# First mixer: norm with one root per token, gate bias loaded early, first projection k by k, five modulation blocks a slab

## The reference

```
def modulate(x, g, shift, scale):
    return rms_norm(x, g) * (1.0 + scale) + shift
...
        mod = (silu_c @ w_mod[l] + b_mod[l]).reshape(B, 3 * N_SUB, 1, D)
        x = macaron_half_ffn(x, norm_g[l, 0], *mod_terms(mod, 0), ffn_w_in[l, 0], ffn_w_out[l, 0])
        sh, sc, gt = mod_terms(mod, 1)
        h = modulate(x, norm_g[l, 1], sh, sc)
...
            y, yx = even_mixer(h, hx, mix_w_in[e], na_rpb[e], ml_gate_b[e], ml_head_g[e], mix_w_out[e], ctx_out)
```

## Time and profile before

| | |
|---|---|
| median of 3 runs | 2561.55 us (2555.28 to 2567.85) |
| the profiled execution | 2558.21 us, its span 2556.4 us |
| PE busy | 2424.2 us, 95% |
| DVE busy | 1718.7 us, 67% |
| ACT busy | 1191.6 us, 47% |
| chain that ended last, by engine | PE 70%, DVE 16%, ACT 9% |
| DMA | 501.16 MB, 196 GB/s on average |

### The profile page before, as it was taken

One profiled execution on the slowest core, in us unless ns is written; L12 is line 12 of the kernel. 1 busy time (PEld: TensorE's weight loads), 2 busy tenths in 40 slices (PEclk: granted clock), 3 DMA queues, 4 the chain that ended last, 5 costly groups with the idle time before them and its releaser, 6 DMA issues.

```text
span 2556.4 us, 34122 instructions
## 1 busy us (share of the span) xinstructions
PE 2424.2 (95%) x14294; PEld 2078.5 (81%) x14294; DVE 1718.7 (67%) x2273; ACT 1191.6 (47%) x1523; POOL 98.9 (4%) x187
## 2 busy tenths in 40 slices
PE   7999999898989999999999999989999899899997
PEld 3778888667789999998899997767777777678776
DVE  5997776653766656655556655577887684678776
ACT  3222222333554544446344444465766644566665
POOL 0111111010000000000000000000000000000000
PEclk9999999999999999999899999999999996999999
DMA  6777787322124545465245542257887521388774
GB/s 274 231 238 263 264 265 252 132 79 94 67 100 167 184 178 179 168 224 191 105 149 177 189 174 102 99 184 271 335 323 293 211 94 53 138 309 329 295 289 175
DMA packets 80386, 501.16 MB, mean 196 GB/s; under 512 B 9605, under 2 KB 10709, under 8 KB 28497
## 3 DMA queue, kind: packets, MB, share of 16 engines
q1 hardware_dynamic: 59120, 423.66, 45.1%
q0 software_dynamic: 21088, 75.01, 9.2%
HBM read 497.58 MB, written 1.05 MB: 195 GB/s over the span
## 4 chain that ended last, share of the span: by engine, by line
PE 70%; DVE 16%; ACT 9%; issue 3%; DMA 2%; ACTq 0%; DVEq 0%; SPq 0%
PE bank L402 68%; DVE wl L1957 7%; ACT wh L1340 6%; DVE macc L1993 1%; ACT s L1438 1%; DVE f L2152 1%; PE bank L613 1%; DVE s L2143 1%; DVE rs L2017 1%; PE bank L1234 1%; DMA raw<-in_wstream 1%; DMA raw<-in_wmod 1%; DMA mring<-in_wmod 1%; DVE hl L2127 0%; ACT H L1447 0%
## 5 line engine op out<-in xcount | busy, mean ns | idle before, releaser
L1957 DVE TENSOR_TENSOR wl<-raw,wh 128x2048 fp32r<-128x2048 f32 (+1 forms) x432 | 903.8, 2097 | 410.7 <-ACT wh L1340 407.8
L1340 ACT ACTIVATE wh<-raw 128x2048 fp32r<-128x2048 f32 (+1 forms) x432 | 755.3, 1756 | 365.2 <-PE bank L402 349.3
L402 PE MATMUL bank<-hh,wh 128*128 128x258 f32 (+2 forms) x2200 | 696.6, 317 | 31.6 <-DVE wl L1957 7.7
L402 PE MATMUL bank<-hh,wl 128*128 128x258 f32 (+2 forms) x2200 | 676.8, 308 | 0.0
L402 PE MATMUL bank<-hl,wh 128*128 128x258 f32 (+2 forms) x2200 | 675.4, 307 | 0.0
L402 PEld LDWEIGHTS bank<-hh,wh 128*128 128x128 f32 x2200 | 424.2, 193 | 62.0 <-DVE hl L2127 8.1
L402 PEld LDWEIGHTS bank<-hl,wh 128*128 128x128 f32 x2200 | 424.8, 193 | 18.5
L402 PEld LDWEIGHTS bank<-hh,wl 128*128 128x128 f32 x2200 | 422.8, 192 | 18.9
L402 PE MATMUL bank<-wh,hh 128*128 128x512 f32 (+1 forms) x704 | 277.9, 395 | 5.5 <-DVE hl L2903 2.8
L402 PE MATMUL bank<-wh,hl 128*128 128x512 f32 (+1 forms) x704 | 273.4, 388 | 0.0
L402 PE MATMUL bank<-wl,hh 128*128 128x512 f32 (+1 forms) x704 | 273.3, 388 | 0.0
(11 more groups left out here) (437 smaller groups left out, 2678.1 us busy)
## 6 DMA issues: line engine op xcount, KB each, us to landing
raw<-in_wstream SPq DMA_DIRECT2D x393, 1024.0 KB, 4.9
mring<-in_wmod POOLq DMA_DIRECT2D x128, 512.0 KB, 4.6
raw<-in_wmod SPq DMA_DIRECT2D x6, 1024.0 KB, 7.1
X<-in_xT SPq DMA_DIRECT2D x1, 2048.0 KB, 12.4
mods<-in_wmod SPq DMA_DIRECT2D x2, 1024.0 KB, 18.9
bias<-in_nabias POOLq DMA_DIRECT2D x16, 128.0 KB, 2.5
c_sglg<-in_sglg POOLq DMA_DIRECT2D x1, 1024.0 KB, 4.5
c_sglb<-in_sglb POOLq DMA_DIRECT2D x1, 1024.0 KB, 6.6
```

Source lines behind the costliest of these rows:

```text
L402: return e.matmul(out, lhsT, rhs, start=start, stop=stop, skip_group_check=True)
L1340: e.activation(wh[i % NB][:, o], raw[i % NR][:, o], ACT.Copy).then_inc(*slab_high(st.split + m))
L1957: e.tensor_tensor(wl[i % NB][:, o], raw[i % NR][:, o], wh[i % NB][:, o].bitcast(F32), ALU.subtract).then_inc(*slab_low(st.split + m))
```

## The change

1. The squares of the mixer's norm are summed with ones as a single column, so that a token's sum stands on its partition (`token_square`, 128x4 in all). `token_inverse` takes mean, root and reciprocal of 128x4, writes them on the diagonal of `rs`, and PE spreads them with one product by ones (`token_roots`). DVE reads the result in its PSUM bank.
2. `naq` is made with k outside: for each k the four column chunks, in four banks.
3. DVE and PE take five modulation blocks at each slab boundary in place of four. All 128 are then through at slab 26 in place of 32, and no sum is left behind the feed-forward.
4. `gateb`, the gates' bias, is loaded with the first constants.
5. ACT's softplus (Abs, Exp, Ln) stands behind the first two of four slab splits, and Ln behind the third.

```
...
@@ -172,6 +172,7 @@
     bmod = const(ctx, "bmod", [P, 2, 72])
     ng = const(ctx, "ng", [P, 7, KC])
     lng = const(ctx, "lng", [P, 8, KC])
+    gate_bias = const(ctx, "gateb", [P, 1])
 
     early = ExitStack()
     macc = sb(early, "macc", [P, 2, 2, D])
...
@@ -421,7 +421,7 @@
             if at == 0:
                 if st.host and i:
                     mod_sums()
-                    mods.advance(4)
+                    mods.advance(5)
                 order.append([])
                 if i:
                     w.wait_ge(slab_low, "slab", i)
@@ -506,14 +506,23 @@
             st.kept.remove(bank_of["ssq", nm])
 
 
-        def first_square(k):
+        def token_square(nm, k):
             if k == 0:
-                st.ssq = bank(("ssq", 0), dve_out, "mean", 0)
+                st.ssq = bank(("ssq", nm), dve_out, "mean", nm)
+                st.kept.add(bank_of["ssq", nm])
                 w.wait_ge(dve_out, "ones")
-            w.wait_ge(act_out, "square", 0, k)
+            w.wait_ge(act_out, "square", nm, k)
             for c in range(4):
                 ins = mm(st.ssq[:, c:c + 1], sq[:, k % 2, P * c:P * c + P], ones[:, 0:1], k == 0 and c == 0, k == KC - 1)
-            ins.then_inc(*result("ssq", 0, k))
+            ins.then_inc(*result("ssq", nm, k))
+            if k == KC - 1:
+                st.kept.remove(bank_of["ssq", nm])
+
+
+        def token_roots(nm, by, *drained):
+            b = bank(("roots", nm), by, *drained)
+            w.wait_ge(dve_out, "diag", nm)
+            mm(b[:], ones[:], rs[:], True, True).then_inc(*result("roots", nm))
 
         def first_mods():
             rows = [bank(("row", i), act_out, "held", i) for i in range(3)]
...
@@ -719,7 +729,12 @@
             def h(k):
                 return h_of(1, 2, k)
 
-            project("min", 4, 0, T, lambda k: h_of(1, 1, k), dve_out, "naq")
+            bs = [bank(("naq", m), dve_out, "naq", m) for m in range(4)]
+            for k in range(KC):
+                w.wait_ge(dve_out, *h_of(1, 1, k))
+                for m, b in enumerate(bs):
+                    wmm(("min", m, k), b[:, 0:T], hh[:, k, 0:T], hl[:, k, 0:T], k == 0, k == KC - 1, "naq", m)
+            st.kept.remove(bank_of["roots", 1])
             project_tok("min", 8, 512, 4, h, act_out, "nav")
 
             def logits(u, kd, qb, hd, b):
@@ -1301,9 +1316,8 @@
         st.host = True
         ffn(1, 0)
         st.host = False
-        mods.advance(200)
-        mod_sums()
-        norm_began(1)
+        token_roots(1, dve_out, "tmp", 1, 2 * KC - 1)
+        st.kept.add(bank_of["roots", 1])
         mixer0()
         ffn(2, 2)
         ffn(3, 3)
...
@@ -1515,15 +1529,16 @@
             w.wait_ge(result, "mixer0 phase 1")
             b = banks[bank_of["mgate", 0]]
             for d in range(2):
-                act(ml.IR[:, d, :], b[32 * d:32 * d + 4, :], ACT.Identity, bias=ml.gb[32 * d:32 * d + 4, :], key=("mgate i", d))
-                act(ml.FR[:, d, :], b[64 + 32 * d:68 + 32 * d, :], ACT.Identity, bias=ml.gb[64 + 32 * d:68 + 32 * d, :],
+                act(ml.IR[:, d, :], b[32 * d:32 * d + 4, :], ACT.Identity, bias=gate_bias[32 * d:32 * d + 4, :], key=("mgate i", d))
+                act(ml.FR[:, d, :], b[64 + 32 * d:68 + 32 * d, :], ACT.Identity, bias=gate_bias[64 + 32 * d:68 + 32 * d, :],
                     key=("mgate", d - 1))
             pad()
+            taken(4 * KC)
             act(ml.t1[:], ml.FR[:], ACT.Abs, key=("softplus", 0))
             act(ml.t1[:], ml.t1[:], ACT.Exp, scale=-1.0, key=("softplus", 1))
+            taken(2 * KC)
             act(ml.t1[:], ml.t1[:], ACT.Ln, bias=1.0, key=("softplus", 2))
-            taken(4 * KC)
-            taken(4 * KC)
+            taken(2 * KC)
             for step in range(4):
                 for d in range(2):
                     ch = seqs[d][step]
@@ -1918,7 +1933,8 @@
         first_mods()
         norm(0, [(0, 0, 1), (2, 0, 1)], ffns[1].tmp)
         ffn(1, 0)
-        root(1, 2 * T)
+        w.wait_ge(dve_out, "mean", 1)
+        e.activation(rt[:], rt[:], ACT.Sqrt).then_inc(*act_out("root", 1))
         norm(1, [(0, 3, 4), (2, 3, 4)], tmpm, 1)
         act_out.mark("mixer0 norm")
         mixer0()
@@ -1963,7 +1979,7 @@
             for i in range(-(-st.tile // 4), -(-(st.tile + n) // 4)):
                 if st.host and i and i % 4 == 0:
                     mod_sums()
-                    for n_ in mods.advance(4):
+                    for n_ in mods.advance(5):
                         mod_block(n_)
                 if st.fine or i % 4 == 0:
                     split_upto(i + 4 * NB - 3 if st.fine else i + 4 * NB)
@@ -2016,6 +2032,17 @@
             for i, o in enumerate(range(0, n, T)):
                 e.reciprocal(rs[:, o:o + T], rs[:, o:o + T]).then_inc(*dve_out("rs", nm, i))
 
+
+        def token_inverse(nm):
+            w.wait_ge(result, "ssq", nm, KC - 1)
+            e.tensor_scalar(rt[:], banks[bank_of["ssq", nm]][:, 0:4], 1.0 / D, 1e-6, ALU.mult, ALU.add).then_inc(*dve_out("mean", nm))
+            w.wait_ge(act_out, "root", nm)
+            e.reciprocal(rt[:], rt[:]).then_inc(*dve_out("inverse", nm))
+            w.wait_ge(const_in["ident"], 0)
+            behind()
+            e.tensor_tensor(rs[:].rearrange("p (b t) -> p b t", b=4), bc(ident[:], 4), rt[:].unsqueeze(2).to_broadcast([P, 4, P]),
+                            ALU.mult).then_inc(*dve_out("diag", nm))
+
         def first_mods():
             e.memset(ones[:], 1.0).then_inc(*dve_out("ones"))
             for k in range(KC):
...
@@ -2104,7 +2124,8 @@
                     behind()
                     e.scalar_tensor_tensor(GV[:, wi, :], mvec(row, scale), 1.0, ng[:, g, :], ALU.add, ALU.mult).then_inc(*dve_out("gv", nm, wi))
             if nm == 1:
-                inv_root(nm, n, 1.0 / D, 1e-6)
+                token_inverse(nm)
+                w.wait_ge(result, "roots", nm)
             U = KC * len(terms)
             if nm == 0:
                 first_norm(terms, tmp)
@@ -2113,11 +2134,13 @@
                 if u < U:
                     wi, k = divmod(u, KC)
                     c = slice(T * wi, T * wi + T)
-                    w.wait_ge(dve_out, "rs", nm, wi)
+                    r = banks[bank_of["roots", 1]] if nm == 1 else rs
+                    if nm != 1:
+                        w.wait_ge(dve_out, "rs", nm, wi)
                     w.wait_ge(dve_out, "gv", nm, len(terms) - 1)
                     if u >= 4:
                         w.wait_ge(dve_out, "hl", nm, u - 4)
-                    e.scalar_tensor_tensor(tmp[:, u % 4, :], X[:, k, c], GV[:, wi, k:k + 1], rs[:, c], ALU.mult,
+                    e.scalar_tensor_tensor(tmp[:, u % 4, :], X[:, k, c], GV[:, wi, k:k + 1], r[:, c], ALU.mult,
                                            ALU.mult).then_inc(*dve_out("tmp", nm, u))
                 if u:
                     wi, k = divmod(u - 1, KC)
@@ -2962,9 +2985,7 @@
         st.host = True
         ffn(1, 0)
         st.host = False
-        for n in mods.advance(200):
-            mod_block(n)
-        mod_sums()
+        assert mods.block == 18 * KC and not mods.ready
         norm(1, 1, [(0, 3, 4), (2, 3, 4)], 2 * T, tmpm)
         dve_out.mark("mixer0 norm")
         mixer0()
@@ -3004,7 +3025,7 @@
             l, term = divmod(g, 9)
             e.dma_start(mring[:, n % NM, :], dram["wmod"][l, P * k:P * k + P, D * term:D * term + D]).then_inc(*mod_in[n % NM](n))
 
-        for name in ("ident", "bmod", "ng", "lng"):
+        for name in ("ident", "bmod", "ng", "lng", "gateb"):
             load(name)
         w.wait_ge(first_in[KC - 1], 0)
         for n in range(2 * KC, 2 * KC + NM):
...
```

91 lines of the change are left out of this document (52 added, 39 removed).

## The result

The changed kernel took 2600.65 us (median of 6 runs, 2589.69 to 2624.55) against 2564.70 us for six runs of the kernel before: a ratio of 1.0131, with an interval of 1.0092 to 1.0171. It is slower, by more than twice what was forecast, and the time lies above the range that was given (2555 to 2586). Its profiled execution took 2596.52 us, against 2558.21 before, so the two traces have 38.3 us between them, and they say where each piece arises. Ratios, and the counts of runs of the kernel before, leave out runs over 1.5% above its fastest on the chip; medians are of all runs.

The account below looks back on a forecast made before the run. PE, busy for 95% of the span, was taken as the bound. From the profiled 2558.2 us, +26 (blocks), -4.4 (roots) and -8.1 (gates) gave 2571.7, stated as 2572 us, range 2555 to 2586.

Parts of the forecast that it names:

- the term for the blocks: First feed-forward: five blocks per slab make DVE late and PE wait, +26 us together.
- The two-vector part: Slabs 1 to 7, blocks of two vectors: PE stands 9 us longer than before.
- The one-vector part: Slabs 8 to 26: late fifth loads cost 20 us, taken as 15, plus group 17's sum, 1.95 us.
- PE's lead: End of the five-block stretch: PE runs ahead, needing only the sums' blocks, and recovers some 4 to 5 us.
- The last rival: Feed-forward: waits pull PE's clock down and loads land late, +20 to +30 us, 2578 to 2590; chance 0.14.
- The roots: Mixer's norm behind the feed-forward: a shorter chain, with the last sum no longer ahead, starts `tmpm` earlier, -4.4 us.
- The projection by k: `naq` behind the norm: stays hidden by ACT's split for slab 35, so 0 us.
- The gates: Behind phase 1 of the mixer: PE's wait at slab 42 and its half clock go, -8.1 us.
- A prompt load: Rival, slabs 8 to 26: the fifth block's load lands in time, about 2559 us, no change; chance 0.20.
- One sign of it: Feed-forward: DVE waiting on `mring` under 1 us for the fifth block would show the forecast wrong.
- most loads land in under 4.6 us: Trace of the kernel before: load times offered as support for the fifth block's load landing in time.
- PE's lead covers the blocks: Rival, feed-forward: PE's slack before each sum makes the extra blocks cost nothing, 2546 us; chance 0.08.

Follow-up runs that it names:

- five_alone: The kernel before with five modulation blocks per slab in place of four, nothing else changed: 2616.43 us, ratio 1.0177.
- after_again: The changed kernel run again unchanged, beside more runs of the kernel before on one chip: 2603.65 us, ratio 1.0100.
- ring4_after: The changed kernel, still five blocks per slab, with a fourth slot for loads of modulation weights: 2571.08 us, ratio 1.0018.
- gates_alone: The kernel before with the gate edits alone (bias resident, slabs split ahead of softplus): 2568.37 us, ratio 0.9998.
- four_rest: The changed kernel with four blocks per slab again, last group's sum behind the feed-forward: 2568.51 us, ratio 1.0005.
- bias_alone: The kernel before with the gates' bias resident, softplus still ahead of the splits: 2576.05 us, ratio 1.0001.
- plan5: four_rest with the last sum beside the roots, three blocks per slab while two-vector, then five, fourth load slot up to block 135: 2558.12 us, ratio 0.9881.
- plan_fill: Like plan5, but five and four blocks in turn, fourth slot up to block 117, six idle 512-column products ahead of the recurrence: 2568.85 us, ratio 0.9934.
- plan5_loop: plan5 with one idle product of 256 columns ahead of each step of the recurrence: 2553.08 us, ratio 0.9870.

## Why the prediction was wrong, step by step

**The sign and the place were right, the size was not.** The blocks were named as the dear part, with DVE's spacing near 16.2 us and near 13.5 afterwards. It was 15.1 to 17.3 (16.1 on average), and 13.6 on average (245.3 us for 18 slabs). But 2600.65 lies outside the range. Two steps failed.

**First, the term for the blocks: +26 forecast, +38.5 in the profile (34.2 in five_alone, 32.8 in after_again).** The two-vector part was put at 9 us and cost 11.1: PE began the first output chunk 15.0 us later, with 3.9 us of sums drawn ahead of it. Slab 7 waited 1.90 and 2.71 us for loads where 1.5 in all had been put in. The one-vector part, with group 17's sum in it, was put at 15 + 2 and cost 27.4. The slab was 13.6 and not 13.4: the spacing was right to 0.2 us. What went wrong was the reckoning with it. I set 13.4 against what PE would need with five blocks (12.35), and then took off 5 us for PE's lead. DVE, however, was at 12.0 per slab before. From slab 7's `f` (17.1 us late) to slab 25's, the last with five blocks ahead of it (45.7 late), it lost 28.6 us; PE recovered 7.2 of these once the blocks were through.

The forecast in the same terms was 15.0 late at slab 7, 24.7 lost behind it (19 slabs at 13.4 in place of 12.1), and so 13.7 recovered: 2.1 for PE's lead at slab 7, 3.9 and 4.75 for sums made earlier, 5 for PE's lead at the end, less 2 for group 17's sum. So of the 12.5 us that are missing 2.1 came at slab 7, 3.9 from DVE's loss behind it, and 6.5, the largest part, from what PE was to recover. The recovery was small in every such profile (7.2, 8.0 in five_alone, 7.3 in after_again); slab 7 was not steady (17.1, 14.4 and 12.1 us late). Behind slab 25 PE has two sums fewer (3.9 us), and loses 2.0 us by the clock of 0.98; which of the credits was false beyond that, no run shows.

The last rival, waits that pull the clock down, named the slow sums rightly (3.8 us in place of 1.95), but they were not what set the time: DVE waited for PE for 0.3 us in that stretch. That the time was above its 2578 to 2590 as well is the recurrence's doing. ring4_after shows that the one-vector part hung on loads issued only three ahead: with a fourth slot it is gone.

**Second, a term that was not in the sum at all: the recurrence's clock, +16.5 in the profile.** The prediction read it nowhere, for the profile of before had it at 1.00. The kernel before itself has the lower clock there in most of its runs, if the mean clocks are read so (56 of the 76 runs of it beside the experiments have one under 0.964); no profile of it shows it. The changed kernel has it in both its profiles, and by the mean clock in all 16 runs. This falls on the comparison, rather than on one edit: five_alone, gates_alone, four_rest, ring4_after, bias_alone and plan5 had it in all six profiles, and by the clock in all 50 runs, whether their gates were changed or not. That the profile of before came from the rarer, quicker kind is bad luck. The kind of fall could have been seen in it, though, in another place: from 2117 to 2161 its clock is at 0.50, in the odd attention. Where like is set against like the change costs 22.7 us, against 13.5 forecast; 33 for the blocks, less 8.3 and 3.6 for the gates and the norm, come to 21. What decides between the two in a run is open: the products and their order in the recurrence are the same in all these kernels. That wide idle products among them hold the clock is shown by plan5_loop; that the narrowness of the recurrence's own is what lets it fall fits this, and fits plan_fill, but is argued, since the same products kept the full clock in other runs.

**The roots: -4.4 forecast, -3.6 found.** The product by ones took 2.05 us, at half clock, and not 1.12; in four_rest it took 1.16. The bigger surprise is in the parts: the roots are worth 1.2 us, and the rest was the sum that edit 3 moved away. The prediction had lumped them.

**The projection by k: 0, right.** From the first product of `naq` to `nav` are 15.5 and 15.4 us in the two kernels, and PE waits 2.54 us for slab 35, within the 2 to 3 that were forecast. It was not run by itself.

**The gates: -8.1 forecast, -8.3 found**, with no wait at slab 42; from 600 to 660 us PE waits for nothing but `kT`, 1.2 us.

**The rivals.** A prompt load fell with the row of 0.98 us on top of 2.13. One sign of it was badly set: a wait of under 1 us for the fifth block was to speak against the forecast, but the forecast's own numbers (a load at 389.4, the fourth block done at 388.65) give a wait of 0.75. And "most loads land in under 4.6 us" misreads a median: half of them do. That PE's lead covers the blocks fell with the 27.4 us of waits for `macc`. The Trainium skill, DMA: Bandwidth & Descriptors, section on the anatomy of one DMA on the gpsimd path, had given an estimate of 3.2 us for such a load. The trace does not agree: the median was 4.6 us in the earlier trace rows, and is 4.8 in the changed kernel's page:

```profile
mring<-in_wmod POOLq DMA_DIRECT2D x128, 512.0 KB, 4.8
```

## What to carry to other kernels

Before giving an engine more pieces per period from a ring, count how many loads must be in flight for them: with three slots the fifth block of a slab waited on its load, and a fourth slot was worth 31 us while the work stayed the same. Compare the new pace with the engine's old pace, and be sparing with what its reader is to recover: of 13.7 us that were credited, 7.2 came. And where a stretch of narrow products shows the full clock in one profile, price it at half clock as well: the mean clock of many runs hints at how often that comes. A few idle full-array products can be cheaper than the fall: in the recurrence they won 10.3 us in the trace, and the whole kernel's median was 5 us lower, which is not clear of the spread.

## What was unexpected of the hardware

TensorE's clock fell to 1.2 GHz for 41 us and more while PE stood idle for nothing in it, in a stretch of 161 products of at most 129 columns, some of them over 4 rows. Idle products of 256 columns over all rows, one ahead of each of 32 steps, made the same stretch 30.1 us at 2.4 GHz in place of 40.4; products of 128 columns made it 27.0. Six products of 512 columns ahead of the stretch, with 32 narrow ones between, changed nothing. The same remedy held the clock in an attention with products of 64 to 256 columns. And one unchanged kernel can be in two groups of runs: plan_fill has four at 2550.1 us or less with mean clocks of 0.967 and more, and six at 2566.7 or more with 0.961 and less. By the same measure the kernel before seems to be in two groups 23 us apart (2558.0 and 2581.0 on one chip), though with no gap between them.
